# A ring of eight landed weight units in the first expert stage of a one-layer decoder step

## The reference

```python
def peer_ffn(h, w_query, sub_keys, expert_u, expert_v):
    xt = h.reshape(n, D)
    q = (xt @ w_query).reshape(n, PEER_HEADS, 2, PEER_DKEY // 2)
    s = jnp.einsum('nhmd,mkd->nhmk', q, sub_keys)
    sv, si = lax.top_k(s, PEER_TOPK)
    cand = (sv[:, :, 0, :, None] + sv[:, :, 1, None, :]).reshape(n, PEER_HEADS, n_cand)
    cidx = (si[:, :, 0, :, None] * PEER_KEYS + si[:, :, 1, None, :]).reshape(n, PEER_HEADS, n_cand)
    fv, fpos = lax.top_k(cand, PEER_TOPK)
    eidx = jnp.take_along_axis(cidx, fpos, axis=-1)
    gate = jax.nn.softmax(fv, axis=-1)
    ...
        act = jax.nn.gelu(jnp.einsum('nd,nhkd->nhk', x_blk, expert_u[i_blk]))
        return jnp.einsum('nhk,nhkd->nd', g_blk * act, expert_v[i_blk])
```

## Time and profile before

| what | value |
|---|---|
| median of 3 runs | 4796.71 us (4792.35 to 4802.76) |
| span of the profiled execution, first to last instruction | 4793.1 us |
| busy PE / DVE / POOL / ACT | 4433.3 / 2599.0 / 2545.3 / 1526.1 us |
| stage A to D, by first and last use of the stage's buffers | about 1869 to 3391 us |
| share of the span of the chain that ended last | PE 4%, issue 1%, others near 0 |

### The profile page before, as it was taken

The page is one execution under the profiler, slowest core; times in us unless marked ns, Lnnn a source line. Parts: engine busy times, 40 slices in busy tenths (PEclk is TensorE's granted clock), DMA queues, the critical chain, the costliest instruction groups (busy, mean ns, idle before and its releaser), DMA issues. The chain is left out here.

```text
span 4793.1 us, 80957 instructions
## 1 busy us (share of the span) xinstructions
PE 4433.3 (92%) x29778; PEld 4169.2 (87%) x29778; DVE 2599.0 (54%) x4336; ACT 1526.1 (32%) x2325; POOL 2545.3 (53%) x1827
## 2 busy tenths in 40 slices
PE   7999968998789898999999999999799999999999
PEld 6888857886379897999988999899799999999889
DVE  4477755453152302679565656555466666666631
ACT  3122214442143323223333333333333333333242
POOL 5688832321034342445566666666566666666543
PEclk9999978998789999999999999999899999999999
DMA  3222222336934432223688988878888888878532
GB/s 110 74 94 94 94 62 89 109 106 229 377 108 134 141 127 68 97 97 130 206 308 310 320 316 310 312 264 311 303 310 325 314 320 313 315 291 321 218 103 93
DMA packets 360238, 985.53 MB, mean 206 GB/s; under 512 B 43218, under 2 KB 120786, under 8 KB 301170
## 3 DMA queue, kind: packets, MB, share of 16 engines
q1 hardware_dynamic: 275138, 566.67, 34.7%
q0 software_dynamic: 47088, 339.37, 18.7%
q10 hardware_dynamic: 37824, 76.99, 4.2%
HBM read 901.03 MB, written 81.82 MB: 205 GB/s over the span
## 5 line engine op out<-in xcount | busy, mean ns | idle before, releaser
L2577 PE MATMUL val_y_ps<-val_wt,val_v 128*128 128x384 f32 x6144 | 1105.3, 338 | 39.2 <-DVE val_wt L2651 21.4
L247 PE MATMUL rt_acc<-xn_act,rt_w_hi 128*128 128x384 f32 x4096 | 1075.0, 343 | 64.0 <-POOL rt_w_rest L237 63.2
L2577 PEld LDWEIGHTS val_y_ps<-val_wt,val_v 128*128 128x128 f32 x6144 | 1065.7, 188 | 78.1 <-DVE out_xT L2675 56.4
L237 POOL TENSOR_TENSOR rt_w_rest<-rt_w_raw,rt_w_hi 128x512 fp32r<-128x512 f32 x576 | 743.4, 1311 | 562.4 <-ACT rt_w_hi L232 559.2
L247 PEld LDWEIGHTS rt_acc<-xn_act,rt_w_hi 128*128 128x128 f32 x4096 | 745.6, 190 | 87.8 <-POOL rt_w_rest L237 84.2
L2539 POOL TENSOR_TENSOR val_v<-val_v_raw,val_v 128x2048 fp32r<-128x2048 f32 x128 | 590.3, 4612 | 367.1 <-ACT val_v L2610 367.1
L247 PE MATMUL rt_acc<-xn_act,rt_w_rest 128*128 128x384 f32 x2048 | 697.0, 340 | 0.0
L232 ACT ACTIVATE rt_w_hi<-rt_w_raw 128x512 fp32r<-128x512 f32 x576 | 345.6, 630 | 494.4 <-DMA rt_w_raw<-in_peer_uT 329.5
L2454 DVE CUSTOM_DVE_ANT_0 rt_space<-rt_space,rt_mid 128x2048 f32<-128x2048 f32 x160 | 361.4, 2280 | 241.8 <-DMA rt_space<-in_peer_u,out_row_id 234.8
L2675 DVE TENSOR_TENSOR out_xT<-out_xT,val_y_ps 128x384 f32<-128x384 f32 x512 | 277.0, 551 | 376.6 <-PE val_y_ps L2577 376.6
L2610 ACT ACTIVATE val_v<-val_v_raw 128x2048 fp32r<-128x2048 f32 x128 | 245.4, 1918 | 583.6 <-PE val_y_ps L2577 551.6
(11 more groups left out here) (404 smaller groups left out, 7234.4 us busy)
## 6 DMA issues: line engine op xcount, KB each, us to landing
rt_w_raw<-in_peer_uT SPq DMA_DIRECT2D x512, 256.0 KB
val_v_raw<-in_peer_vp SPq DMA_DIRECT2D x128, 1024.0 KB, 4.9
scan_w_raw<-in_w_in SPq DMA_DIRECT2D x128, 256.0 KB, 3.0
pages_V<-in_cache_v SPq DMA_DIRECT2D x64, 512.0 KB, 11.8
att_w_raw<-in_w_in SPq DMA_DIRECT2D x96, 256.0 KB, 3.3
hid_scratch<-rt_hid ACTq DMA_DIRECT2D x128, 192.0 KB
gate_scratch<-rt_space ACTq DMA_DIRECT2D x12, 2048.0 KB
val_hid<-hid_scratch SPq DMA_DIRECT2D x32, 768.0 KB
```

The source lines that it names most:

```text
L237: e.tensor_tensor(self.rest[:, s, 0:nk, :], self.raw[:, s, 0:nk, :], self.hi[:, s, 0:nk, :].bitcast(F32), ALU.subtract).then_inc(self.rest ...
L247: mm = e.matmul(acc[:, h, 0:width], w[:, s, k, :], act[:, kt0 + k, a, col + h * width:col + (h + 1) * width], start=first and k == 0 and w ...
L2577: mm = e.matmul(y_ps[:, t % 2, 0:DW], v[:, c % 2, a, j, t * P:(t + 1) * P], wt[:, g % 2, j, b, :], start=j == 0 and a == 0 and b == 0, sto ...
```

## The change

`Stream` takes a depth for `raw` and its landing semaphores; the expert stage passes 8. `hi` and `rest` keep four slots. `load` for unit u now waits for the subtraction of unit u - 8. Since stage A has 12 units in a round, which eight does not divide, the loops over its rounds on SP and ACT become unrolled code. Room for the eight slots comes from `keysT` and `more_id`, `more_gate`, which move into the stage's shared area, and from tables of 384 columns in place of 544. As `more_id` and `more_gate` now lie where `out` is written, ACT waits for their eight DMAs to land before it starts stage C.

```diff
-    def __init__(self, s):
-        self.raw = s.sb("w_raw", [P, RING, UNIT, P])
+    def __init__(self, s, depth=RING):
+        self.depth = depth
+        self.raw = s.sb("w_raw", [P, depth, UNIT, P])
         self.hi = s.sb("w_hi", [P, RING, UNIT, P], F32R)
         self.rest = s.sb("w_rest", [P, RING, UNIT, P], F32R)
-        self.landed = s.sems("w_landed", RING)
+        self.landed = s.sems("w_landed", depth)
...
     def load(self, e, i, per, u, src):
         e.wait_ge(self.rest_done, i * per + (u + 1))
+        s = u % self.depth
+        e.dma_start(self.raw[:, s, 0:src.shape[1], :], src).then_inc(self.landed[s], 16)
+
+    def split_hi(self, e, i, per, u, nk=UNIT):
+        s, r = u % RING, u % self.depth
+        e.wait_ge(self.landed[r], i * (16 * (per // self.depth)) + 16 * (u // self.depth + 1))
+        e.wait_ge(self.used, i * per + (u + 1))
+        e.activation(self.hi[:, s, 0:nk, :], self.raw[:, r, 0:nk, :], ACT.Copy).then_inc(self.hi_done, 1)
...
-        e.wait_ge(self.rest_done, i * per + (RING + u + 1))
+        e.wait_ge(self.rest_done, i * per + (self.depth + u + 1))
...
     def credit_rest(self, e):
-        e.sem_inc(self.rest_done, RING)
+        e.sem_inc(self.rest_done, self.depth)
...
-        w = Stream(s)
+        w = Stream(s, 2 * RING)
...
-        tables = s.sb("tables", [P, 3, TOK])
-        keysT = s.sb("keysT", [P, 2, P])
+        tables = s.sb("tables", [P, 3, DW])
...
+        keysT = ranks.take(2, P)
...
-        more_id = s.sb("more_id", [EX, HK], U32)
-        more_gate = s.sb("more_gate", [EX, HK])
+        more_id = out[0:EX, :, :].rearrange("p j n -> p (j n)")[:, 0:HK].bitcast(U32)
+        more_gate = out[0:EX, :, :].rearrange("p j n -> p (j n)")[:, HK:2 * HK]
...
-            with e.Fori(0, T_A) as i:
+            for i in range(T_A):
...
-                    w.load(e, i, PER_A, u, src)
+                    w.load(e, 0, 0, i * PER_A + u, src)
...
-                    w.split_hi(e, i, PER_A, u)
+                    w.split_hi(e, 0, 0, i * PER_A + u)
...
-            queries(0, True)
-            with e.Fori(1, T_A) as i:
-                queries(i, False)
+            for i in range(T_A):
+                queries(i, i == 0)
...
             for u in range(2):
                 w.split_hi(e, 0, 0, base(FIRST_C) + u)
+            e.wait_ge(more_in, 2 * 16 * (P // EX))
...
-                ch.did(e.tensor_copy(tables[:, t, 0:NP], end[:, 0, :]))
-                ch.did(e.tensor_copy(tables[:, t, NP:TOK], end[:, 1, 0:NS]))
+                ch.did(e.tensor_copy(tables[:, t, 0:NP - D0], end[:, 0, D0:NP]))
+                ch.did(e.tensor_copy(tables[:, t, NP - D0:DW], end[:, 1, 0:NS]))
...
-                n0 = D0 + m * BT
+                n0 = m * BT
```

More of the change, by code:

```diff
@@ L224, in load @@
         e.wait_ge(self.rest_done, i * per + (u + 1))
-        s = u % RING
+        s = u % self.depth
         e.dma_start(self.raw[:, s, 0:src.shape[1], :], src).then_inc(self.landed[s], 16)
     def split_hi(self, e, i, per, u, nk=UNIT):
-        s = u % RING
-        e.wait_ge(self.landed[s], i * (16 * (per // RING)) + 16 * (u // RING + 1))
+        s, r = u % RING, u % self.depth
+        e.wait_ge(self.landed[r], i * (16 * (per // self.depth)) + 16 * (u // self.depth + 1))
         e.wait_ge(self.used, i * per + (u + 1))
-        e.activation(self.hi[:, s, 0:nk, :], self.raw[:, s, 0:nk, :], ACT.Copy).then_inc(self.hi_done, 1)
+        e.activation(self.hi[:, s, 0:nk, :], self.raw[:, r, 0:nk, :], ACT.Copy).then_inc(self.hi_done, 1)
     def split_rest(self, e, i, per, u, nk=UNIT):
-        s = u % RING
+        s, r = u % RING, u % self.depth
         e.wait_ge(self.hi_done, i * per + (u + 1))
-        e.tensor_tensor(self.rest[:, s, 0:nk, :], self.raw[:, s, 0:nk, :],
+        e.tensor_tensor(self.rest[:, s, 0:nk, :], self.raw[:, r, 0:nk, :],
                         self.hi[:, s, 0:nk, :].bitcast(F32), ALU.subtract).then_inc(self.rest_done, 1)
```

## The result

The changed kernel takes 4742.9 us (median of 4 runs, 4738.9 to 4750.3) against 4797.2 in the same comparison: ratio 0.9886, 95% interval 0.9874 to 0.9899, 54 us less.

The account below looks back on a forecast made before the run. Only stage C could gain: PE waited 54.7 us for POOL's remainder, mostly behind late weight landings. Terms -27.4 - 4.5 - 12 + 10 = -33.9 took the median from 4796.7 to 4763 us, range 4745 to 4790 (8 in 10).

Parts of the forecast that it names:

- clock: Stage C: seven narrow windows of lowered PE clock cost 15 us; -12 of it, bounds 0 and 15.
- landing stalls: Stage C: 20 PE stalls that began at a late weight landing, 31.4 us, fall to 4: -27.4.
- ACT's order: Stage C, mostly a chunk's first tile: 13 PE stalls behind ACT's `finish`, gate copies and store, 10.0 us; -4.5.
- dot stalls: Stage C: 12 PE stalls from late dot products, 13.0 us, grow to 23: +10, bounds 0 and +15.
- new wait on ACT: Start of stage C: ACT stands 1.3 us for eight small DMAs, hidden behind POOL's gather: nothing; upper bound some 6 us.
- the term for what is late next: Stage C, DVE and POOL: PE stalls from late dot products grow from 13.0 to 23 us: +10.
- the five stalls that were to come down to 0.45 us: Stage C: five PE stalls, 6.8 us together, where ACT reached `finish` late after waiting for a landing; -4.5.
- its floor, 51 us: Stage C, best case: -31.4 - 4.5 - 15 = -51, 4746 us; better than forecast by over 10 us had chance 0.06.
- DMA is the bound: Stage C: if DMA engines bear at most 0.88 busy, C shrinks only 11 us: 4786 us; chance 0.15.
- DVE and POOL give most of it back: Stage C: all 29 batches stall and the lowered clock stays, so -17: 4780 us; chance 0.12.
- Gathers come late: Stage C: more queued weight packets delay each gather; at 1.5 us each it is +18: 4815 us; chance 0.07.
- Slots that do not fill: Stage C: were POOL late in releasing loads, SP would run no further ahead; chance included in "DMA is the bound".

Follow-up runs that it names:

- experiment 10: The changed kernel with a ring of six and SP's and ACT's loops over tiles and chunks fully unrolled: 4746.7 us, 0.9892 of the kernel before.
- experiment 1: The changed kernel run again with no edit: 4742.7 us, 0.9886 of the kernel before.
- experiment 9: The changed kernel, ring of eight, with only ACT's loop over chunks made three chunks a turn: 4760.3 us, 0.9919 of the kernel before.
- Experiment 7: The changed kernel with gathers 3 to 127 two units later and ACT rounding three units ahead, not two: 4712.0 us, 0.9818 of the kernel before.
- experiment 3: The changed kernel with a ring of four and stage C's gate stores replaced by same-size stores in stage A: 4749.4 us, 0.9896 of the kernel before.
- experiment 2: The changed kernel with a ring of four, all its other edits kept: 4796.4 us, 0.9995 of the kernel before.
- experiment 5: The changed kernel with a ring of six, ACT's loop three chunks and SP's six tiles a turn: 4762.7 us, 0.9925 of the kernel before.

## Why the prediction fell short

The mechanism stood in the main: where the kernel lost time, what the ring takes away and what is late next were each found where the prediction had put them. The sizes of the terms were off, nearly all to one side. They account for 12 of the 20 us that the forecast missed; the other 8 stood in no term (see below). The measured column follows every stall of the changed kernel back as the prediction did for the one before; the clock is half the length of the stretches at the lower level.

| term | forecast | measured in the trace |
|---|---|---|
| landing stalls | 31.4 to 4: -27.4 | 31.4 to 0: -31.4 |
| ACT's order | -4.5 | 10.0 to 5.7: -4.3 |
| clock | -12 of 15 | -15, no lowered stretch left in C |
| dot stalls | 13.0 to 23: +10 | 13.0 to 17.7 in 18 places: +4.7 |
| new wait on ACT | 1.3 us, hidden | 1.1 us, hidden |
| sum | -34 | -46 |

**The step that failed** is the term for what is late next, "I take 23: +10", and the caution put on the two others beside it: of the 12 us, 5.3 lie in the dot stalls, 4 in the landings left over and 3 in the clock. A second step failed with it, the cost of a stall taken as the idle printed between matmuls (see the rest of the difference). The growth was derived from two schedules, which gave 29 places if every batch were long. Batches did not grow long everywhere once landings were in time: of 48, 18 took 5 us or more before, and 25 in the change. Two places of the changed kernel, DVE, POOL and PE (compare rows 6):

```profile
2466.31 6.09 DVE L2447 TENSOR_SCALAR rt_space<-all_const,rt_tables 128x128 f32<-128x128 f32 x8
...
2474.88 0.95 POOL L2138 DMA_INDIRECT rt_space<-in_peer_u,out_row_id  x1 [2.57 <-DVE out_row_dot L2455]
...
2477.18 0.62 PE L248 MATMUL rt_acc<-xn_act,rt_w_hi 128*128 128x384 f32 x2 [1.52 <-POOL rt_w_rest L238]
```

```profile
2546.22 5.12 DVE L2447 TENSOR_SCALAR rt_space<-all_const,rt_tables 128x128 f32<-128x128 f32 x8
...
2556.14 0.61 PE L248 MATMUL rt_acc<-xn_act,rt_w_hi 128*128 128x384 f32 x2 [0.57 <-POOL rt_w_rest L238]
```

A batch of 6.1 us gives a stall of 1.52 and one of 5.1 gives 0.57, a microsecond for a microsecond; of eleven batches of 4.1 to 4.2 us ten give none. The place counts too: one of 7.4 us, at 2446.72, gives 0.70, and the one of 4.11 us behind the batch at 2466.31 gives 1.66. So the input, that a fed POOL makes every batch long, was wrong; that the schedules' arithmetic was right is not shown for each place. With the loops written out and a ring of six (experiment 10), 35 of 48 batches take 5 us or more, and 25 such stalls of 21.8 us appear, near the forecast's 23 us. That the lengths come from the port pair that VectorE and GpSimd share, as the Trainium skill (SBUF — State Buffer, "Who interferes with whom") has it, agrees with 6.1 beside 2.1 us; no run took the lock away, so it stays argued.

**Two readings in ACT's order.** Of the five stalls that were to come down to 0.45 us, four did; in place of the 1.34 us one at 3255.91 the change has 1.40 us at 3214.27, with no landing ahead of it (0.41 in the repeat of experiment 1), so the ring does not account for that one. And the stalls of 0.45 us at the chunk starts were laid to ACT's order, that is `finish`, copies and store. Part of them is the turn of ACT's loop: from the store's issue to the next rounding ACT needs 0.86 us in the change and 0.43 written out (experiment 10), in the same order, and with that these stalls are gone; at the chunk starts of experiment 9 that have no turn they are 0.15 us at most.

**The rest of the difference.** The terms sum to -46, the first expert stage became 51 us shorter from trace to trace (its last dense matmul starts 3389.8 - 1914.2 = 1475.6 us after the first before, 3343.8 - 1919.4 = 1424.4 after), and the medians differ by 54. PE's idle as printed between matmuls does not hold all that a stall costs: the weight loads' waits behind the remainder fell from 74.8 to 42.1 us, and to 34.3 without the passage into C, so by 40, where the matmuls' fell by 31. The prediction took its floor, 51 us, from the matmul row alone, and so set the lower end of the range 2 us too high. Experiment 7, which has no such stall, tells how much the row lacks: its eleven chunks take 828.8 us, so those of before cost 77.5 us more and those of the change 29.9. Idle printed between matmuls (less the 1.4 us that experiment 7 has too) and lost clock explain 50.5 + 15.4 of the first and 21.4 of the second. That leaves 11.6 us over 40 stalls and 8.5 over 26, 0.2 to 0.3 us a stall beyond what is printed. With 17 stalls fewer in the stage (46 to 29) this makes up most of the 5 us between 46 and 51. The last 3 us, from 51 to the 54 of the medians, are within the scatter of executions.

**The rivals.** *DMA is the bound*: wrong; 0.89 in the change and 0.92 in experiment 7. The 158 waits for landings spoke for it; in experiment 3 there are 161, and they began only 5.7 us of stalls. *DVE and POOL give most of it back*: they gave back 4.7 us, and no lowered clock followed. *Gathers come late*: DVE's wait for them fell from 234.8 to 202.0 us, and a gather of the change lands 8.2 us after its issue (median of 147 in stage C), where 9.5 us to its dot was the sign. By the rule of the Trainium skill (DMA: Bandwidth & Descriptors, "Queues, rings and completion order") that an engine takes its queues in turn, packet by packet, a deeper queue costs a gather packet one weight packet at most; the trace does not speak against it, but no run shows the arbiter. *Slots that do not fill*: ACT's waits for landings went from 329.5 to none. The room's edits: nothing, as forecast (experiment 2).

## What to carry to other kernels

Size a prefetch ring by the longest late landing that the consumer must ride out, not by the sum of its waits: 307 us of landing waits began only 5.7 us of stalls once the 2 MB burst was gone, and a ring of four with the burst lost 54. When a ring lifts one limit, follow each remaining stall to its start; here two shifts in orders written by hand gave 31 us more. And do not discount every term of a sum for caution, when each is read from rows: the errors add up. The idle printed between matmuls was less than what a stall cost, by 0.2 to 0.3 us each.

## What the runs showed of the hardware that was not expected

A loop of ACT whose body is three chunks long stopped ACT for 5.3 to 6.4 us at each of its turns, on no semaphore, and PE for 4.5 to 5.7. From a chunk's store to the next rounding ACT needs 5.1 to 6.2 us at such a turn, 0.86 with one chunk a turn, and 0.43 written out. Code that must be fetched anew is a possible cause, and is not shown: an 8 KB packet of the instruction queue falls into each of the six stops (the first at 2584.4 us in experiment 5), but the unrolled kernels have such packets without a stop, and the trace does not say for which engine one is.

The seven stretches of lowered clock in stage C of the kernel before came with PE stalls of 1.76 us and more, while all 18 dot stalls of up to 1.66 us in the change left it at 1.00. The length of a stall alone does not tell, though: three stalls of 2.09, 2.67 and 3.07 us of the kernel before (at 2852.66, 3343.31 and 2524.54) were followed by a clock of 1.00.
